# Rounding the weights on ScalarE, key tiles ahead of value tiles, and eight buffers for the squares, in a two-layer hybrid decoder trunk

## The reference

```python
def _layer(x, ...):
    h = _rmsnorm(x, norm_attn)
    z = h @ w_in                       # split into gq, gk, gv, ga, gg, sq, sk, sv
    o_gla = gated linear attention of 4 heads, normalized, times silu(gg)
    o_swa = windowed softmax attention of 8 query heads over 2 key heads,
            with rotary positions and a sink logit per head; cached keys for the samples
    x = x + concat([o_gla, o_swa]) @ w_o
    h = _rmsnorm(x, norm_ffn)
    x = x + (silu(h @ w_gate) * (h @ w_up)) @ w_down        # inner width 2816
```

## Time and profile before

| | |
|---|---|
| median of 3 runs | 2575.66 us (2574.88 to 2577.61) |
| the profiled execution | 2577.41 us |
| its span | 2575.6 us |
| mean granted clock of TensorE | 0.975 |
| busy: TensorE, VectorE, GpSimd, ScalarE | 2465.1, 1183.5, 946.7, 545.7 us |

### The profile page before, as it was taken

How to read it: one execution, slowest core, us unless ns; L and a number is a source line. 1 busy time by engine, 2 the same in 40 slices (tenths; PEclk the granted TensorE clock), 3 DMA queues, 4 the chain that set the end, 5 groups by cost and what they waited for, 6 DMA issues and landing times.

```text
span 2575.6 us, 38958 instructions
## 1 busy us (share of the span) xinstructions
PE 2465.1 (96%) x15280; PEld 2363.4 (92%) x15280; DVE 1183.5 (46%) x2267; ACT 545.7 (21%) x1344; POOL 946.7 (37%) x1413
## 2 busy tenths in 40 slices
PE   5999999999999999999988999999999999999997
PEld 5886888999999999999987777899999999999996
DVE  4646574333343343434565566652343333343345
ACT  4025454210000000000320454432000000000002
POOL 6222212634343433334552212145343434343434
PEclk8999998999999999999998999989999999999998
DMA  4200101211111111111131001021111111111112
GB/s 163 95 25 25 42 18 69 66 42 42 49 41 48 45 44 49 41 49 41 59 124 36 25 26 42 19 92 42 50 41 49 41 49 41 49 42 47 48 42 76
DMA packets 47237, 130.99 MB, mean 51 GB/s; under 512 B 4288, under 2 KB 21888, under 8 KB 46336
## 3 DMA queue, kind: packets, MB, share of 16 engines
q1 hardware_dynamic: 38208, 110.91, 13.2%
q10 hardware_dynamic: 8928, 18.71, 2.0%
HBM read 117.18 MB, written 14.45 MB: 51 GB/s over the span
## 4 chain that ended last, share of the span: by engine, by line
PE 88%; DVE 5%; POOL 2%; ACT 2%; issue 2%; DMA 0%; ACTq 0%; SPq 0%; DVEq 0%; POOLq 0%; PEldq 0%
PE acc L632 17%; PE acc L633 17%; PE acc L634 16%; PE pair_a L632 7%; PE pair_a L633 7%; PE pair_a L634 7%; PE single L633 3%; PE single L632 3%; PE single L634 3%; POOL sums L577 1%; PE pair_b L786 1%; PE pair_a L814 1%; PE single L797 1%; PE pair_a L774 1%; PE acc L864 1%
## 5 line engine op out<-in xcount | busy, mean ns | idle before, releaser
L546 POOL TENSOR_TENSOR w_hi<-w_raw,const 128x32 fp32r<-128x32 f32 x186 | 51.9, 279 | 1493.1 <-PE acc L634 860.4
L554 POOL TENSOR_TENSOR w_lo<-w_raw,w_hi 128x256 fp32r<-128x256 f32 x744 | 549.5, 769 | 15.5
L632 PE MATMUL acc<-h_hi,w_hi 128*128 128x384 f32 (+1 forms) x1200 | 412.1, 343 | 32.3 <-POOL w_lo L554 23.4
L633 PE MATMUL acc<-h_lo,w_hi 128*128 128x384 f32 (+1 forms) x1200 | 400.6, 334 | 0.0
L634 PE MATMUL acc<-h_hi,w_lo 128*128 128x384 f32 (+1 forms) x1200 | 398.8, 332 | 0.0
L632 PE MATMUL acc<-f_hi,w_hi 128*128 128x384 f32 (+1 forms) x1056 | 343.6, 325 | 3.1 <-PEq L917 3.1
L633 PE MATMUL acc<-f_lo,w_hi 128*128 128x384 f32 (+1 forms) x1056 | 341.3, 323 | 0.0
L634 PE MATMUL acc<-f_hi,w_lo 128*128 128x384 f32 (+1 forms) x1056 | 340.1, 322 | 0.0
L632 PEld LDWEIGHTS acc<-h_hi,w_hi 128*128 128x128 f32 x1200 | 235.8, 196 | 49.4 <-POOL w_lo L554 21.6
L1664 DVE TENSOR_TENSOR silu_g<-acc,sums 128x384 f32<-128x384 f32 x132 | 69.3, 525 | 410.5 <-PE acc L634 397.9
L1266 ACT ACTIVATE silu_g<-silu_g 128x384 f32<-128x384 f32 x132 | 65.7, 499 | 890.1 <-DVE silu_g L1664 890.1
(11 more groups left out here) (240 smaller groups left out, 4718.7 us busy)
## 6 DMA issues: line engine op xcount, KB each, us to landing
w_raw<-units SPq DMA_DIRECT2D x186, 512.0 KB, 3.4
park<-x ACTq DMA_DIRECT2D x2, 2640.0 KB, 18.5
x<-park ACTq DMA_DIRECT2D x2, 2640.0 KB, 10.1
y_t<-x SPq DMA_DIRECT2D x4, 768.0 KB, 4.5
rope<-tables SPq DMA_DIRECT2D x2, 1056.0 KB, 9.2
s<-state_in ACTq DMA_DIRECT2D x4, 512.0 KB, 5.7
state_s<-s SPq DMA_DIRECT2D x2, 1024.0 KB, 5.5
x<-x_t SPq DMA_DIRECT2D x2, 768.0 KB, 5.7
```

The source lines that it names most:

```text
L546: nc.gpsimd.tensor_tensor(w_hi[:, s, 0:SUB], w_raw[:, s, 0:SUB], c_("ones")[:, 0:SUB], ALU.mult)
L554: low = nc.gpsimd.tensor_tensor(w_lo[:, s, a:a + LOW], w_raw[:, s, a:a + LOW], w_hi[:, s, a:a + LOW].bitcast(f32), ALU.subtract)
L632: nc.tensor.matmul(out, wh, hi, start=first, stop=False)
L633: nc.tensor.matmul(out, wh, lo, start=False, stop=False)
```

## The change

Four things are changed together.

- **Rounding.** A new step `("round", u)` lets ScalarE make `w_hi` by two copies of 512 columns. It waits for the load, and for TensorE's last use of the slot. In the hand-written order it stands behind the last tile of the unit that used the slot (`take` of tile 2); in the feed-forward `next_unit` stands behind the Silus, behind the hidden copies, and behind the down units. GpSimd's `split` keeps the four subtractions and waits only for ScalarE.
- **Order.** In both layers the three key tiles come first, then the three value tiles. The sums (`stat`) move with them. The first two query tiles come before the third tile's sum, its key and value takes, and the third query tile. One projection (`rest[0]`) now stands before the decode scores, and two instead of one behind each decode scores; the items begin at projection 7 of the list instead of 4.
- **Squares.** `square_slot` gives the squares of the layer's first norm, and of the last norm, eight buffers (`sqr0`, over memory that the queries and keys of the linear attention use later).
- **Start.** The key unit is loaded first and the constants behind the third tile. GpSimd waits for the constants only behind the first two units' splits, and splits the third unit between the first and second tiles' sums of squares.

```diff
-SQR = 2
+SQR, SQR0 = 2, 8
...
+    z = [("z", u, tt) for u in (U_SK, U_SV) for tt in range(NTT)]
     if l == 0:
-        steps += [("halves", 0), ("squares", 0, 0), ("halves", 1), ("halves", 2)]
-    z = [("z", u, tt) for tt in range(NTT) for u in (U_SK, U_SV)]
-    steps += z[:3] + [("stat", 0)] + z[3:5] + [("stat", 1), z[5], ("stat", 2)]
-    if l == 0:
-        steps += evacuated(0) + [("squares", 1, 0)] + evacuated(1) + [("squares", 2, 0)] + evacuated(2)
+        steps += [("round", U_SK), ("halves", 0), ("squares", 0, 0), ("round", U_SV), ("halves", 1), ("halves", 2)]
+        steps += z[:4] + [("stat", 0)] + z[4:] + [("stat", 1), ("round", U_SQ)]
+        steps += [("squares", 1, 0)] + evacuated(0) + [("squares", 2, 0)] + evacuated(1)
     else:
-        steps += [("squares", 1, LATE)] + evacuated(0) + [("squares", 2, LATE)] + evacuated(1) + evacuated(2)
-    steps += [("turn_v", U_SV, 0), ("turn_v", U_SV, 1), ("park",)]
...
+        steps += z[:2] + [("stat", 0)] + z[2:4] + [("stat", 1)] + z[4:]
+        steps += evacuated(0) + [("squares", 1, LATE), ("squares", 2, LATE), ("round", U_SQ)] + evacuated(1)
+    q = U_SQ
+    steps += project(q, 0) + [("round", q + 1)] + project(q, 1) + [("turn_v", U_SV, 0), ("turn_v", U_SV, 1), ("stat", 2)]
+    steps += evacuated(2) + project(q, 2) + [("park",)]
...
-    steps.append(("turn_k",))
+    steps += [("turn_k",)] + rest[0]
     for g in range(2):
-        steps += [("dec_scores", g)] + rest[2 * g] + [("dec_norm", g), ("dec_turn", g)] + rest[2 * g + 1]
-        steps += [("dec_values", g)]
+        a, b, c = rest[1 + 3 * g:4 + 3 * g]
+        steps += [("dec_scores", g)] + a + b + [("dec_norm", g), ("dec_turn", g)] + c + [("dec_values", g)]
     items = 2 * NCH
-    first = done = 4
+    first = done = 7
...
-    return steps
+    out = []
+    for s in steps:
+        out.append(s)
+        if s[0] == "take" and s[1] >= U_SQ and s[2] == NTT - 1:
+            out.append(("round", s[1] + RING))
+    return out
...
+    def square_slot(a):
+
+        if a < NADDED:
+            return sqr0[:, a % SQR0, :], a - SQR0 + 1
+        return sqr[:, (a - NADDED) % SQR, :], a - SQR + 1 if a >= NADDED + SQR else 0
...
+            load(0, U_SK)
             for k in range(2):
                 kk = slice(KC // 2 * k, KC // 2 * (k + 1))
                 sp.dma_start(x[:, kk, cols(0)], x_t[:, kk, cols(0)]).then_inc(x_in[k], 16)
                 if k == 0:
-                    load(0, U_SK)
                     sp.dma_start(par[:, 0:NPARAM], params[0]).then_inc(L[0].par_loaded, 16)
-                    sp.dma_start(const[:], consts).then_inc(set_up, 16)
+            sp.dma_start(x[:, :, cols(1)], x_t[:, :, cols(1)]).then_inc(x_in[2], 16)
             load(0, U_SV)
-            sp.dma_start(x[:, :, cols(1)], x_t[:, :, cols(1)]).then_inc(x_in[2], 16)
             sp.dma_start(x[:, :, cols(2)], x_t[:, :, cols(2)]).then_inc(x_in[3], 16)
+            sp.dma_start(const[:], consts).then_inc(set_up, 16)
...
-            def split(l, u, loads, high):
+            def split(l, u, high):
 
                 S = L[l]
                 s = slot(l, u)
-                pool.wait_ge(S.w_loaded[u % RING], loads)
-                nc.gpsimd.tensor_tensor(w_hi[:, s, 0:SUB], w_raw[:, s, 0:SUB], c_("ones")[:, 0:SUB],
-                                        ALU.mult)
-                nc.gpsimd.tensor_scalar(w_hi[:, s, SUB:UNIT // 2], w_raw[:, s, SUB:UNIT // 2], 1.0, 0.0,
-                                        ALU.mult, ALU.add)
-                nc.gpsimd.tensor_scalar(w_hi[:, s, UNIT // 2:], w_raw[:, s, UNIT // 2:], 1.0, 0.0,
-                                        ALU.mult, ALU.add).then_inc(S.w_high, 1)
                 pool.wait_ge(S.w_high, high)
...
-            pool.wait_ge(set_up, 16)
             unit(0, U_SK)
             unit(0, U_SV)
+            pool.wait_ge(set_up, 16)
             for tt in range(NTT):
                 for k in range(KC):
                     add(L[0], ADDED[0], BLOCK[0], (0, k, tt))
+                if tt == 0:
+                    unit(0, U_SQ)
...
+            def rounded(l, u, loads):
+
+                S, s = L[l], slot(l, u)
+                act.wait_ge(S.w_loaded[u % RING], loads)
+                nc.scalar.activation(w_hi[:, s, 0:UNIT // 2], w_raw[:, s, 0:UNIT // 2], ACT.Copy)
+                nc.scalar.activation(w_hi[:, s, UNIT // 2:], w_raw[:, s, UNIT // 2:], ACT.Copy).then_inc(S.w_high, 1)
...
+                    if s[0] == "round":
+                        u = s[1]
+                        if u >= U_SQ + RING:
+                            act.wait_ge(S.acc_full, GROUP[("z", u - RING, NTT - 1)] + 1)
+                        elif u >= RING:
+                            act.wait_ge(S.head_full, head_done(u - RING, NTT - 1))
+                        rounded(l, u, 16 * (u // RING + 1))
...
+                def next_unit(i, j, groups):
+
+                    u = U_FF + j
+                    act.wait_ge(S.acc_full, i * FF_GROUPS + (G_FF + groups))
+                    rounded(l, u, i * (16 * FF_UNITS // RING) + 16 * (u // RING + 1))
```

More of the change, by code:

```diff
@@ L212, in group_numbers, with rope_takes @@
     return table, n
+def rope_takes(steps):
+    return [s for s in steps if s[0] == "take" and (s[1] == U_SK or U_SQ <= s[1] < U_GK)]
 def count_before(steps, kind, step):
@@ L454, in head_bank, with head_done @@
         return 2 * tt + (u - U_SK)
+    def head_done(u, tt):
+        return NTT * (u - U_SK) + tt + 1
     def slot(l, u):
@@ L567, in unit @@
             def unit(l, u):
-                split(l, u, 16 * (u // RING + 1), u + 1)
+                split(l, u, u + 1)
             def add(S, table, order, b):
@@ L577, in add @@
                     nc.gpsimd.tensor_tensor(sums[tt][:, 0:width(tt)], sums[tt][:, 0:width(tt)],
[L578 to L580 removed]
+                                            square_slot(a)[0][:, 0:width(tt)], ALU.add).then_inc(S.sq_added, 1)
             unit(0, U_SK)
             unit(0, U_SV)
+            pool.wait_ge(set_up, 16)
             for tt in range(NTT):
@@ L585, in _ @@
                     add(L[0], ADDED[0], BLOCK[0], (0, k, tt))
-            ends = [NTT * (j + 1) for j in range(4)] + [4 * NTT + 4 * NTT * (j + 1) for j in range(2)]
-            before = [ends[4] - FF_GROUPS, ends[5] - FF_GROUPS] + ends[0:4]
+                if tt == 0:
+                    unit(0, U_SQ)
             for l in range(DEPTH):
-                S, GROUP = L[l], GROUPS[l]
+                S = L[l]
                 def added(k, tt):
                     add(S, ADDED[l], BLOCK[l], (1, k, tt))
-                for u in range(RING, U_FF + RING):
+                for u in range(RING + 1 if l == 0 else RING, U_FF + RING):
                     if u >= U_WO + RING:
@@ L608, in _ @@
                 for j in range(RING, FF_UNITS):
-                    pool.wait_ge(S.acc_full, G_FF + before[j])
                     unit(l, U_FF + j)
@@ L613, in _ @@
                         u = U_FF + j
-                        pool.wait_ge(S.acc_full, i * FF_GROUPS + (G_FF + before[j]))
-                        split(l, u, i * (16 * FF_UNITS // RING) + 16 * (u // RING + 1), i * FF_UNITS + (u + 1))
+                        split(l, u, i * FF_UNITS + (u + 1))
                 sums_of = L[l + 1] if l + 1 < DEPTH else F
@@ L714, in _ @@
                         open_group(g)
-                        pe.wait_ge(S.roped, NTT)
+                        pe.wait_ge(S.roped, rope_takes(steps).index(("take", U_SK, NTT - 1)) + 1)
                         nc.tensor.transpose(bank(g)[:, 0:P], ks[:, SEQ - P:SEQ], c_("ident"))
@@ L992, in square @@
                     else:
-                        if a >= SQR:
-                            act.wait_ge(S.sq_added, a - SQR + 1)
-                        dst = sqr[:, a % SQR, 0:w]
+                        dst, done = square_slot(a)
+                        if done > 0:
+                            act.wait_ge(S.sq_added, done)
+                        dst = dst[:, 0:w]
                     nc.scalar.activation(dst, x[:, k, cols(tt)], ACT.Square).then_inc(S.squares, 1)
@@ L1006, in _ @@
                 for s in steps:
-                    if s[0] == "halves":
+                    if s[0] == "round":
[5 more added lines that the diff above has]
+                        rounded(l, u, 16 * (u // RING + 1))
+                    elif s[0] == "halves":
                         _, tt = s
@@ L1278, in ff_pass @@
                                                  ACT.Copy).then_inc(S.hid_high, 1)
+                        next_unit(i, RING + 2 * f + 1, NTT * (2 * f + 2))
+                    if not final:
+                        for j in range(2):
+                            next_unit(i, FF_UNITS + j, 4 * NTT + 4 * NTT * (j + 1))
                 def block_left(n):
@@ L1299, in _ @@
                                 square(L[l + 1], ADDED[l + 1][(0, kk, 0)], kk, 0)
+                        if n + 1 in (4 * NTT, 8 * NTT):
+                            u = U_SK + (n + 1) // (4 * NTT) - 1
```

(4 more changed lines are left out.)

23 lines of the change are left out of this document (12 added, 11 removed).

## The result

The changed kernel takes 2541.28 us (median of 4 runs, 2540.92 to 2545.35) beside 2575.28 for the kernel before: a ratio of 0.987, 95% interval 0.9853 to 0.9887. Forecast were 2549 and a range of 2537 to 2566, so the sign and the range held, and the gain is 34 us where 26 were forecast. The profiled execution took 2540.92, with a span of 2539.1 against 2575.6: 36.5 us to account for.

A forecast was written before the change was run, and what follows sets the result against it. TensorE, busy 96% of the span, was taken as the bound. Layer 0's start 4, layer 1's start 10 and the attentions 12 sum to 26 us off, giving 2549.7 at the median; forecast 2549, range 2537 to 2566.

The forecast's parts named there:

- start of layer 0: First layer's start: key unit loaded first brings the first matmul and first query tile earlier; 4 us gained, bounds -3 to 11.
- start of layer 1: Second layer's start: keys' tiles first remove the waits for the value split and turned value tile; 10 us, bounds 7 to 12.
- The attention: Decode scores and softmax items: projection tiles moved from the items' loop fill stands; 6 us a layer, bounds 2 and 10.
- edits put at nothing: Eight square buffers in the last norm, rounds in gated stage and output projection, later loads: nothing, bounds together -4 to +1 us.
- 0.86: Time in us taken for one h_lo on VectorE beside a GpSimd split in layer 0's start; alone 0.53.
- new stand of 1.7: Layer 1's start: TensorE newly waits 1.7 us for the second query tile's bank.
- The attention gives nothing: Rival, chance 0.17: items' loop bound by VectorE's and ScalarE's chain, each tile taken out returns as a stand; 2562 us.
- The start gains more: Rival, chance 0.13: constants land before the third tile, so layer 0's start gains 7 us more; 2542 us.
- Slower: Rival, chance 0.07: in the attention, rounds waiting on ScalarE hold back probability copies; 31 us if all on the path, 2580.
- 22 rounds on the path: Number of the attention's 26 rounds, 1.2 us each, on the path from which the slower rival decides.
- VectorE and GpSimd exclude each other: Rival, chance 0.08: in layer 0's start eleven h_lo take about 1.5 us, key tiles end at 42, layer loses 2; 2555.

The follow-up runs named there:

- e4: Changed kernel with the first tile's squares behind all halves in layer 0's start and the second unit's round behind the second tile's halves; 2531.33 us.
- e6: Changed kernel with only the load of the constants moved, from behind the third tile's to behind the first tile's first half; 2535.35 us.
- e9: Changed kernel with one step moved: in layer 0's start the second unit's round stands in front of the first tile's squares; 2536.05 us.
- e7: Changed kernel with only the rounding put back on GpSimd; order, loads, buffers and tiles stay as changed; 2540.13 us.
- e1: Kernel before with only the rounding moved to ScalarE; in layer 1 the third unit's round stands in front of the squares; 2572.65 us.
- e8: e1 with layer 1's third-unit round behind the second and third tile's squares instead of in front; 2565.47 us.
- e2: Kernel before with only the projection tiles placed anew: one before the decode scores, two and one behind each, three fewer in the items' loop; 2554.63 us.
- e10: e4 with a unit's round in the attention behind the next copy of transposed probabilities (one unit of seven: behind the exponentials); 2526.36 us.

## Why the prediction was right, and where its sizes were off

The sum came out near because misses cancelled in part: the start of layer 0 was 4 us too high, the two attentions together 8 too low and the gated stages 6 too low; only the start of layer 1 was right in size. The attention (10.2 a layer, bound 10) and the edits put at nothing (6 in all, bound 1) lie above their own bounds. That the time stayed well inside the range is in part luck: without the miss of the first start it would have lain at the lower edge, near 2537.

*Start of layer 0 (4, measured 0).* Most instants held: first matmul 8.78 (forecast about 10), first tile's end 15.65 (15.6), squares from 17.87 (18.0), halves of the second tile from 22.22 (22.9), the stand until 23.59 (24.3). Then the sizes failed. Key tiles ended at 39.14, not 36.4: the 16 low halves took 14.5 us, where eleven at 0.86 and five at 0.53 make 12.1, and the granted clock was 0.76 from 23.60 to 39.20. The first query tile came at 52.4, not 49.4, and the third ended at 72.2, not 65.8, since it ran at half clock behind its stand (0.52 from 66.20 to 72.40). The mechanism I had named, the constants' wait with the halves behind it, was right (e4, e6). That the second unit's round behind it costs 4.5 us (e9) I had not seen.

*Start of layer 1 (10, measured 10.4).* Right in size, and the new stand of 1.7 too. My reason named three rounding instructions fewer along with the order; e7 shows that they are worth 1 us here, and e1 and e8 that rounds without the new order lose 12 and 5.

*Attention (6 a layer, measured 10).* The idle time of the decode stretch fell from 9.6 to 4.7 (42.4 long, 32.76 busy; after 44.0 and 39.27), forecast 5.3 left. The step that was mis-sized is "about 6 of the busy time is half clock; I let half of it go": with 11.8 us of tiles added the stretch should be 44.6 busy and is 39.3, so 5.3 went and the clock is 1.00. In the items' stretch I put 2.5 back for stands of VectorE's norm in four items. The idle time did rise, from 6.9 to 8.8, but VectorE's share fell (4.6 to 2.1 in the layer) and ScalarE's probability copies rose (1.9 to 6.5), and the last half clock there went as well (mean 0.99 to 1.00), so only 0.4 came back (144.8 against 156.2 - 11.8). e2 shows that the places of the tiles make this gain by themselves.

*Edits at nothing (0, measured 3 a layer).* Right for the feed-forward: 788.8 and 788.8, with two copies of 0.624 us a unit on ScalarE and no wait for a split weight there. Wrong for the gated stage, which I called ScalarE's idle time without asking what GpSimd's shorter chain gives VectorE. Eight buffers were said to gain nothing in the last norm, which holds; in layer 0, with e4's order, two lengthened the start by 3.5 to 5.6 us (100.6 against 95.0 and 97.1), of which the median shows 2.5.

*Rivals.* "The attention gives nothing" fell by e2. "The start gains more" fell as a forecast, as the constants came last (17.87); what it supposed gives 7 us of the key turn when it is made true (e6). "Slower" was there in kind, not in size: rounds in front of probability copies cost 2.3 us a layer (e10), far from 22 rounds on the path.

*"VectorE and GpSimd exclude each other"* was right in kind; its price was too high, and the 0.86 by which I set it aside was misread. Taken one at a time, instructions of the changed kernel go in turn:

```profile
24.09 1.04 POOL L573 TENSOR_TENSOR w_lo<-w_raw,w_hi 128x256 fp32r<-128x256 f32 x1
24.46 1.08 DVE L1369 SCALAR_TENSOR_TENSOR h_lo<-x,par,h_hi 128x384 fp32r<-128x384 f32 x1
25.09 1.04 POOL L573 TENSOR_TENSOR w_lo<-w_raw,w_hi 128x256 fp32r<-128x256 f32 x1
25.47 1.09 DVE L1369 SCALAR_TENSOR_TENSOR h_lo<-x,par,h_hi 128x384 fp32r<-128x384 f32 x1
...
28.86 1.14 POOL L596 TENSOR_TENSOR sums<-sums,sqr 128x384 f32<-128x384 f32 x1
29.05 1.36 DVE L1369 SCALAR_TENSOR_TENSOR h_lo<-x,par,h_hi 128x384 fp32r<-128x384 f32 x1
30.14 1.13 POOL L596 TENSOR_TENSOR sums<-sums,sqr 128x384 f32<-128x384 f32 x1
```

Each of these low halves ends some 0.41 us behind the end of a GpSimd instruction (25.13 and 25.54, 30.00 and 30.41), and the next GpSimd instruction ends behind the low half. Eleven low halves let GpSimd's eleven instructions pass, as the rival had it. The Trainium skill ("SBUF — State Buffer", SBUF: two separate sides) says that whoever comes first holds the shared pair for a whole instruction and the other fully blocks; these rows agree, one instruction for one. But a turn of both takes 1.00 us with a subtraction and 1.28 with a sum, not 1.5: less than the two times alone, 0.53 and 2.77 / 4 = 0.69 (e9) for low half and subtraction. The key tiles ended at 39.14, between my 36.4 and the rival's 42. My 0.86 was a mean over eight low halves, of which the last four, beside the subtractions, were 1.00 us apart.

The 8.51 of the earlier trace rows is not the time alone either. Its second low half met the last sum:

```profile
25.69 1.30 POOL L577 TENSOR_TENSOR sums<-sums,sqr 128x384 f32<-128x384 f32 x1
26.04 1.37 DVE L1327 SCALAR_TENSOR_TENSOR h_lo<-x,par,h_hi 128x384 fp32r<-128x384 f32 x1
```

Its neighbours took 0.6, so all 16 alone take about 7.7, an estimate. By that, 12.1 us of GpSimd's work (22.86 to 34.92) lengthened them by 6.8 in the changed kernel, and 5.5 us (22.13 to 27.67) by 3.3 in e9: VectorE lost a little over half of the overlap.

## What to carry to other kernels

Where work is handed from one engine to another, ask what it will be queued behind on the new one: here rounds gave 3 us a layer where ScalarE was idle, and cost 4.5 behind a wait for a late load and 2.3 a layer in front of a copy that TensorE wants. Independent tiles put into the stands of the decode stretch gave back 4.9 us of idle time and, as much again, 5.3 of half clock, so price a stand by both. Two engines that share a chain are best judged by putting one back alone: here the part named first in the change was worth nothing in sum, the places of the tiles made most of the gain, and the order, by elimination, most of the rest. And a mean over several instructions can hide that two engines take turns: look at the ends of single ones.

## What the runs showed of the hardware

TensorE's busy time was worth 17.2 of the 36.5 us: 2465.1 us before and 2447.9 after, on the same 15280 matmuls, with a mean granted clock of 0.975 and 0.985. In the decode stretch of the earlier trace rows four stands of 9.6 us in sum went with a clock of 0.84, four of 4.7 with 1.00. One and the same start took 95.0 and 97.1 us in two kernels, by busy time alone. And VectorE's low halves and GpSimd's instructions went in turn, 1.00 us for a low half with a subtraction and 1.28 with a sum: 16 low halves took about 7.7 us alone (an estimate), 11.0 beside part of the sums (e9) and 14.5 beside split and sums.
